# Up and gate products of six MLPs as seven block products (Strassen) in place of eight

## The chip, the cores and the metric

The kernel runs on one core of one Trainium2 chip. The metric is the time of one execution in microseconds of device time. A profile of one execution stands beside the times; its rows are shown below.

## The reference

Four layers over 512 tokens of width 1024, in float32. The change touches the feed-forward parts only. Cut to these:

```python
# first two layers, i = 0, 1 (width of the MLP 4096)
h = _layer_norm(DN_ALPHA * h + y, ln1_g[i], ln1_b[i])
u = jnp.square(jax.nn.relu(h @ mlp_w1[i])) @ mlp_w2[i]
h = _layer_norm(DN_ALPHA * h + u, ln2_g[i], ln2_b[i])
h = h + jax.nn.sigmoid(h @ ple_gate_w[i]) * (p[i] @ ple_w[i])
...
# last two layers (width 2816), a gated MLP ahead of and behind the mixer
def _swiglu(x, w_gate, w_up, w_down):
    return (jax.nn.silu(x @ w_gate) * (x @ w_up)) @ w_down
x = x + MACARON * _swiglu(_rmsnorm(x, ffn1_norm), ffn1_w_gate, ffn1_w_up, ffn1_w_down)
```

So there are six stages of the kind: two plain MLPs and four gated ones. The mixers (attention, retention and others) lie between them and stay as they are.

## The kernel before

**Split products.** TensorE multiplies in a short float format (`float32r`). To keep float32 accuracy every operand is split into a high part (ScalarE copies it into that format) and a low part (the rest, value minus high part), and each product is three matmuls: high x high, low x high, high x low. `mm3` (lines 431 to 434) issues them. In the up and gate products (`fm`, lines 468 to 493; `fm_product`, lines 459 to 466) the weights are the stationary operand, 128 x 128, and x, transposed, moves with 512 tokens as columns: one PSUM bank holds 128 features of 512 tokens. In the down products (`tm`, lines 511 to 546) the activations are stationary and the weights move.

**Weights.** `weight_plan` lists all weight tiles in the order of use, 128 x 2048 numbers (1 MB) each as a rule: 256 features of 1024 inputs for up and gate, 512 outputs of 512 inputs for down. Tile j goes through slot j % 2 of the buffers `wraw`, `whi` and `wlo`. SyncE's queue loads it (`load`, lines 2694 to 2706) when the old tenant has been split; ScalarE writes the high part (line 1065) when TensorE has used tile j - 2; GpSimd writes the low part (line 2541), and of a few tiles VectorE writes half (line 1652). `Slots.prepare` does this one tile ahead (`LOOK = 1`): the split of tile j + 1 has the time in which TensorE works on tile j.

**An MLP stage.** The hidden width is cut into chunks of 8 tiles of 128 features (`chunks`); the last chunk of the gated MLP has 6. For a chunk, first all up (and gate) products are made, then its down products, whose sum is added to the residual `h` by VectorE (lines 1761, 1763). Plain MLP: ScalarE applies relu on the way out of PSUM (line 1367), VectorE squares (line 2110), ScalarE makes the high part `uh` (line 1371), VectorE the low part `ul` (line 2112). Gated MLP: ScalarE applies silu to the gate's bank (line 1409), VectorE multiplies by the up product's bank (line 2150), then high part (line 1414) and low part (line 2152).

**Start of a stage.** The normed x has to be transposed: TensorE transposes 128 tokens (line 451), ScalarE and VectorE write `xh` and `xl` (lines 1084, 1701). `Handover` orders this around the last products of the stage before. So that work can start early, the first two weight tiles (four feature tiles) are multiplied with tokens 0 to 255 first and with 256 to 511 after that, as matmuls with 256 columns.

**The per-layer input.** GpSimd loads `p` (line 2603) at the start of a plain MLP, ScalarE and VectorE split it after the first chunk (lines 1381, 2122), and its products (`ple`) stand right behind the last down product; they cover the norm.

All engines run in the order in which their program issues; waits are semaphore waits written by name (`at(...)`).

Of the kernel before, what the change touches and what calls it, by code (L numbers as in the profile page):

```python
# [19 lines left out]
SLOT = 2048  # L20
NRAW, NSPL, LOOK = 2, 2, 1
# [13 lines left out]
FINAL = 13  # L35

# [74 lines left out]
class Slots:  # L111


    def __init__(self, plan, split):
        self.plan, self.split, self.i, self.ahead = plan, split, 0, 0

    def prepare(self):
        while self.ahead <= min(self.i + LOOK, len(self.plan) - 1):
            self.split(self.ahead)
            self.ahead += 1  # L120

    def get(self, tag, later=0):
        assert self.plan[self.i + later][0] == tag, (self.plan[self.i + later][0], tag)
        self.prepare()
        return self.i + later
# [64 lines left out]

def weight_plan(I):

    plan, shared = [], {0}
# [5 lines left out]
    def add_fm(tag, v, c0, c1, step=256):  # L199
        for c in range(c0, c1, step):  # L200
            plan.append((tag, v[:, :, c:min(c + step, c1)]))

    def add_tm(tag, v, c0, c1, early=False):
        nk = v.shape[1]
        for c in range(c0, c1, 512):
            for k, kn in k_parts(nk):
                plan.append((tag, v[:, k:kn, c:min(c + 512, c1)]))
        if early:
            n = len(plan) - 2
# [4 lines left out]
    plan.append(("e_g", v[:, :, 3328:3424]))  # L214
    add_fm("e_vs", v, 1024, 1280)
    for j in range(2):
        plan.append(("cmp", I["e_b_cmp_w1"][j].rearrange("p (k c) -> p k c", c=128)))
        add_fm("e_qk", v, 1280 + 256 * j, 1536 + 256 * j)
        shared.add(len(plan) - 1)
    n = len(plan)  # L220
# [4 lines left out]

    def plan_mlp(i):
        v1, v2 = kview("mlp_w1", i), kview("mlp_w2", i)
        parts = chunks(DFF // 128)
        for a, b in parts:
            add_fm("up", v1, a * 128, b * 128)  # L230
# [4 lines left out]
    def plan_glu(g, u, d, l):  # L235
        vg, vu, vd = kview(g, l), kview(u, l), kview(d, l)
        parts = chunks(DFF2 // 128)
        for a, b in parts:
            for c in range(a, b, 2):
                add_fm("glu", vg, c * 128, c * 128 + 256)  # L240
                add_fm("glu", vu, c * 128, c * 128 + 256)
            add_tm("down", vd[:, a:b, :], 0, D, (a, b) == parts[-1])

# [9 lines left out]
    for l in range(2):  # L253
        plan_glu("ffn1_w_gate_2", "ffn1_w_up_2", "ffn1_w_down_2", l)
# [6 lines left out]
        plan_glu("ffn2_w_gate_2", "ffn2_w_up_2", "ffn2_w_down_2", l)  # L261
    return plan, shared
# [6 lines left out]
def memory(nc, k):  # L269
# [13 lines left out]
    k.hi = [sb(f"whi{i}", [128, SLOT], R) for i in range(NSPL)]  # L283
    k.lo = [sb(f"wlo{i}", [128, SLOT], R) for i in range(NSPL)]
# [28 lines left out]
    def mlp(i):  # L313
        with ExitStack() as sc:
            def tmp(name, shape, dt=F):
                return sc.enter_context(nc.sbuf_tensor(f"{name}_m{i}", shape, dt))
            s = Kit()
            s.uh, s.ul = tmp("uh", [128, 8, T], R), tmp("ul", [128, 8, T], R)
            s.sg, s.pb = tmp("sg", [128, 4, 512]), tmp("pb", [128, 4, D])
            s.tb = tmp("tb", [128, 3, T])  # L320
            s.ph, s.pl = tmp("ph", [128, 2, T], R), tmp("pl", [128, 2, T], R)
            s.pr = tmp("pr", [128, 2, T])
            if i == 0:
                s.posi, s.posf, s.ang = tmp("posi", [128, NT], I32), tmp("posf", [128, NT]), tmp("ang", [128, 3, NT, 48])
# [26 lines left out]
    def glu(l, which):  # L351
        with ExitStack() as sc:
            def tmp(name, shape, dt=F):
                return sc.enter_context(nc.sbuf_tensor(f"{name}_g{l}{which}", shape, dt))
            s = Kit()
            s.uh, s.ul = tmp("uh", [128, 8, T], R), tmp("ul", [128, 8, T], R)
            s.tb = tmp("tb", [128, 4, T])
            return s

# [19 lines left out]
    k.mlp = {0: mlp(0)}  # L379
    k.odd = odd()  # L380
    k.zt = sb("zt", [128, 2, D])
    k.mlp[1] = mlp(1)
    k.glu = {(l, w): glu(l, w) for l in range(2) for w in (1, 2)}
# [3 lines left out]
def signals(nc, k, v):  # L387
# [8 lines left out]
    for n in range(NRAW):  # L396
# [3 lines left out]
def slot_views(k, j):  # L400
    kt, c = k.plan[j][1].shape[1:]
    return [x[j % NSPL][:, 0:kt * c].rearrange("p (k c) -> p k c", c=c) for x in (k.hi, k.lo)]


def split_views(k, j):
    kt, c = k.plan[j][1].shape[1:]
    return k.raw[j % NRAW][:, 0:kt * c], k.hi[j % NSPL][:, 0:kt * c], k.lo[j % NSPL][:, 0:kt * c]


def whole(k, j):  # L410
    return k.plan[j][0] == "cmp"


def glu_slots(a, b):
    return [(c, part) for c in range(a, b, 2) for part in ("g_gate", "g_up")]


def tensor_program(nc, k):
# [4 lines left out]
    slots = Slots(k.plan, lambda j: None)  # L423
# [7 lines left out]
    def mm3(o, lh, ll, rh, rl, start, stop):  # L431
        M.matmul(o, lh, rh, start=start, stop=False)  # L432
        M.matmul(o, lh, rl, start=False, stop=False)  # L433
        return M.matmul(o, ll, rh, start=False, stop=stop)  # L434

    def weights(j):
        pe.wait_ge(at("lo", j))
# [16 lines left out]
    def turned(tt):  # L454
        pe.wait_ge(at("xl", ho.round, tt))
# [38 lines left out]

    def tm_part(j, kr, bank, key, tt, src, nk, need, n, turns=True, last=False):
# [4 lines left out]
        for kk in range(*kr):  # L500
            if need:
                pe.wait_ge(at(*need(kk)))
# [76 lines left out]
    def even():  # L579
# [20 lines left out]
        def hidden(n):  # L600
            j = slots.get("cmp")
            pe.wait_ge(at("raw", j))
            pe.wait_ge(at("windows", n))
            w = k.raw[j % NRAW][:, 0:SLOT].rearrange("p (k c) -> p k c", c=128)
# [152 lines left out]

    def mlp(i):
        s = k.mlp[i]
# [2071 lines left out]
```

## Time and profile before

| | |
|---|---|
| Runs | 3649.26 us median of three (3648.98 to 3652.57) |
| Profiled execution | 3641.17 us, its span 3639.8 us |
| TensorE | 3467.6 us busy, 95% |
| VectorE, ScalarE, GpSimd | 1290.6, 1076.8, 1225.0 us busy (35%, 30%, 34%) |
| Mean granted TensorE clock | 0.974 of full |
| DMA | 308 MB, 85 GB/s |

Matmuls overlap: each is listed from its start to its modelled end, so the pace is read from one start to the next. "PEld" are the loads of the stationary operand. A row of idle time names what ended it.

### The profile page before, as it was taken

What the parts mean: (1) busy time and instruction counts of PE and PEld (TensorE: products, weight loads), DVE (VectorE), ACT (ScalarE), POOL (GpSimd) and SP (SyncE); (2) the same over time, 40 slices, a digit from 0 to 9 for tenths busy, and PEclk for the clock granted to TensorE, in tenths of its full rate; (3) what the DMA queues carried; (4) which work ended last, traced back from release to release, by engine and by line L of the source; (5) the groups of instructions that cost most, each with busy time, mean ns of one, the idle gap of its engine ahead of it and who ended that gap; (6) DMA issues with size and microseconds to landing.
All of it is one profiled execution on the core that took longest, in us unless ns stands there. A gap on an engine that the chain in (4) does not pass through costs nothing.

```text
span 3639.8 us, 37569 instructions
## 1 busy us (share of the span) xinstructions
PE 3467.6 (95%) x16220; PEld 2795.4 (77%) x16220; DVE 1290.6 (35%) x2250; ACT 1076.8 (30%) x1431; POOL 1225.0 (34%) x343
## 2 busy tenths in 40 slices
PE   7999999999879999999999999999999999999998
PEld 6775688887655888877888777888788877778887
DVE  3446533244682522252111546111221115461112
ACT  3453322223432232243222222222232222223222
POOL 3210134432421344423443332344334433323442
PEclk9989999999879999999999999999999999999999
DMA  4210123322110233222232321223222323222222
GB/s 155 85 47 1 37 97 97 112 78 91 52 41 25 86 104 104 93 87 81 93 109 82 105 93 58 93 93 110 82 93 93 98 84 117 77 70 93 93 99 81
DMA packets 221142, 308.33 MB, mean 85 GB/s; under 512 B 6096, under 2 KB 149472, under 8 KB 220464
## 3 DMA queue, kind: packets, MB, share of 16 engines
q1 hardware_dynamic: 217920, 293.50, 25.0%
q0 software_dynamic: 3056, 12.42, 0.9%
q8 instruction: 128, 2.10, 0.2%
q14 instruction: 38, 0.31, 0.0%
HBM read 303.80 MB, written 2.10 MB: 84 GB/s over the span
## 4 chain that ended last, share of the span: by engine, by line
PE 83%; DVE 11%; ACT 3%; POOL 2%; issue 1%; DMA 0%; ACTq 0%; DVEq 0%; POOLq 0%
PE bank L432 25%; PE bank L434 25%; PE bank L433 25%; ACT whi L1065 2%; POOL wlo L2541 2%; PE bank L734 1%; PE bank L705 1%; DVE wkk_o L2290 1%; DVE uv_x L2419 1%; PE bank L908 1%; DVE wlo L1652 1%; DVE gb L2287 1%; PE bank L719 1%; PE bank L451 1%; DVE tb_m L2110 1%
## 5 line engine op out<-in xcount | busy, mean ns | idle before, releaser
L2541 POOL TENSOR_TENSOR wlo<-wraw,whi 128x2048 fp32r<-128x2048 f32 (+2 forms) x279 | 1186.9, 4254 | 2189.4 <-ACT whi L1065 2189.4
L432 PE MATMUL bank<-xh,whi 128*128 128x512 f32 (+1 forms) x2456 | 922.6, 376 | 52.7 <-POOL wlo L2541 19.8
L434 PE MATMUL bank<-xh,wlo 128*128 128x512 f32 (+1 forms) x2456 | 917.7, 374 | 0.0
L433 PE MATMUL bank<-xl,whi 128*128 128x512 f32 (+1 forms) x2456 | 917.5, 374 | 0.0
L1065 ACT ACTIVATE whi<-wraw 128x2048 fp32r<-128x2048 f32 (+1 forms) x279 | 519.4, 1861 | 885.5 <-PE bank L434 854.2
L432 PEld LDWEIGHTS bank<-xh,whi 128*128 128x128 f32 x2456 | 466.9, 190 | 150.0 <-POOL wlo L2541 32.0
L434 PEld LDWEIGHTS bank<-xh,wlo 128*128 128x128 f32 x2456 | 466.7, 190 | 90.0
L433 PEld LDWEIGHTS bank<-xl,whi 128*128 128x128 f32 x2456 | 467.2, 190 | 88.7
L432 PE MATMUL bank<-whi,xh 128*128 128x512 f32 (+2 forms) x976 | 377.9, 387 | 22.7 <-POOL wlo L2541 9.6
L433 PE MATMUL bank<-wlo,xh 128*128 128x512 f32 (+2 forms) x976 | 371.6, 381 | 0.0
L434 PE MATMUL bank<-whi,xl 128*128 128x512 f32 (+2 forms) x976 | 371.1, 380 | 0.0
L1763 DVE SCALAR_TENSOR_TENSOR h<-bank,h 128x512 f32<-128x512 f32 x160 | 110.5, 690 | 588.1 <-PE bank L434 588.1
L2150 DVE TENSOR_TENSOR tb_g<-tb_g,bank 128x512 f32<-128x512 f32 x88 | 60.4, 687 | 716.2 <-PE bank L434 713.5
L432 PE MATMUL bank<-whi,uh_g 128*128 128x512 f32 x704 | 274.7, 390 | 5.6 <-POOL wlo L2541 5.6
L434 PE MATMUL bank<-whi,ul_g 128*128 128x512 f32 x704 | 274.0, 389 | 0.0
L433 PE MATMUL bank<-wlo,uh_g 128*128 128x512 f32 x704 | 273.9, 389 | 0.0
L432 PEld LDWEIGHTS bank<-whi,xh 128*128 128x128 f32 x976 | 188.7, 193 | 64.6 <-POOL wlo L2541 13.1
L434 PEld LDWEIGHTS bank<-whi,xl 128*128 128x128 f32 x976 | 188.1, 193 | 36.2
L433 PEld LDWEIGHTS bank<-wlo,xh 128*128 128x128 f32 x976 | 188.5, 193 | 34.3
L432 PE MATMUL bank<-whi,uh_m 128*128 128x512 f32 x512 | 199.9, 390 | 2.1 <-POOL wlo L2541 1.8
L434 PE MATMUL bank<-whi,ul_m 128*128 128x512 f32 x512 | 199.3, 389 | 0.0
L433 PE MATMUL bank<-wlo,uh_m 128*128 128x512 f32 x512 | 199.2, 389 | 0.0
(344 smaller groups left out, 3318.4 us busy)
## 6 DMA issues: line engine op xcount, KB each, us to landing
wraw<-in_mlp_w SPq DMA_DIRECT2D x64, 1024.0 KB, 5.3
wraw<-in_ffn_w_gate SPq DMA_DIRECT2D x44, 1024.0 KB, 5.4
wraw<-in_ffn_w_up SPq DMA_DIRECT2D x44, 1024.0 KB, 5.4
wraw<-in_ffn_w_down SPq DMA_DIRECT2D x40, 1024.0 KB, 5.1
wraw<-in_w_in SPq DMA_DIRECT2D x26, 1024.0 KB, 5.2
wraw<-in_e_w_in SPq DMA_DIRECT2D x13, 1024.0 KB, 5.5
wraw<-in_ple_gate_w SPq DMA_DIRECT2D x8, 1024.0 KB, 5.4
wraw<-in_w_out SPq DMA_DIRECT2D x8, 1024.0 KB, 5.0
```

Source lines behind the costliest of these rows:

```text
L432: M.matmul(o, lh, rh, start=start, stop=False)
L433: M.matmul(o, lh, rl, start=False, stop=False)
L434: return M.matmul(o, ll, rh, start=False, stop=stop)
L451: i = M.transpose(bank[:, j * 128:(j + 1) * 128], src[:, (f + j) * 128:(f + j + 1) * 128], ident)
L705: M.matmul(bank[:, 0:nk], lq, e.kvT[ps, 1 + br, 0:nk], start=True, stop=False)
L719: ins = M.transpose(bank[0:w, o:o + 128], e.P[:, (n % 2) * 2 + h, kk:kk + w], ident)
L734: ins = M.matmul(o[:, 0:256], lhs, rhs, start=(br == 0), stop=(br == 2 and kk + 128 >= nk))
L908: M.matmul(bank[:, 0:nk], o.qr[ps, hh // 2, s], o.krT[ps, 0:nk], start=False, stop=False)
L1065: A.activation(hi, raw, ACT.Copy).then_inc(*k.w_hi.inc(("hi", j)))
L1763: V.scalar_tensor_tensor(x, y, scale_y, x, ALU.mult, ALU.add).then_inc(*done.inc(*names))
L2150: V.tensor_tensor(t, t, ring.of(key)[:, :], ALU.mult).then_inc(*done.inc(("gu", g, f), ("free", key)))
L2541: G.tensor_tensor(lo[:, 0:n], raw[:, 0:n], hi[:, 0:n].bitcast(F), ALU.subtract).then_inc(*k.w_lo.inc(("lo", j)))
```

## The change

For a block of 2n feature tiles, x is cut into four quarters (two halves of the 1024 inputs by two halves of the 512 tokens) and the weights into four (two halves of the inputs by two of the features). Seven products of sums of quarters replace the eight products of quarters, in Winograd's form. A *unit* is one such block: n is 2 (four feature tiles), and 1 for the last two tiles of the gated MLP. Each of the seven products of a unit is n x 4 x 3 matmuls with 256 columns.

- *Sums of x* are made once for each stage, after all its tokens are transposed: `operands()` on VectorE (four sums, five low parts) and ScalarE (high parts). There are now seven operand pairs `x[0..6]`.
- *Sums of weights*: VectorE, in place in the raw buffer, four for each unit (`weight_sum`). The low parts of five of the seven weight operands move to VectorE; GpSimd keeps products 2 and 3 (and 1 in the two first units of a stage).
- *Buffers*: high and low buffers are four halves of 1024 columns, one for each product; a whole slot (down weights and all others) takes two. There are two more raw buffers while an MLP stage runs.
- *Partial sums* stay in PSUM where the next product adds to them. ScalarE copies a bank out in between (`snap`), and VectorE adds the later bank to the copy (`add_bank`).
- *Square* moves from VectorE to ScalarE. The load of `p` moves behind the last low part of `u`.

```diff
+OPERAND = {1: 4, 2: 5, 3: 3, 4: 6, 5: 0, 6: 1, 7: 2}
+SNAP = {1: "11", 5: "22", 6: "12"}
+SUM = {2: "11", 7: "22", 3: "12"}
+ON_POOL = (2, 3)
+def product_order(n, start):
+    steady = [(u, p) for u in range(n) for p in (1, 5, 6, 2, 7, 3, 4)]
+    if not start:
+        return steady
+    return [(0, 1), (0, 2), (1, 1), (1, 2), (0, 5), (0, 6), (1, 5), (0, 7), (1, 6), (0, 3), (0, 4), (1, 7), (1, 3), (1, 4)] + steady[14:]
...
 class Slots:
     def prepare(self):
-        while self.ahead <= min(self.i + LOOK, len(self.plan) - 1):
+        while self.ahead < len(self.plan) and max(self.plan[self.ahead].before, default=-1) < self.i:
...
+    def item(self, tag, load, n, unit=None, p=None):
+        if n == 2:
+            self.half += self.half % 2
+        halves = [(self.half + i) % 4 for i in range(n)]
+        self.half = (self.half + n) % 4
+        before = sorted({self.split_at[x] for x in halves if x in self.split_at})
...
+    def unit_sizes(a, b):
+        return [(f, 2 if f + 4 <= b else 1) for f in range(a, b, 4)]
...
 # TensorE
+    def units(tag, blocks):
...
+        for n, (i, p) in enumerate(product_order(len(blocks), start)):
+            u = blocks[i]
+            j = slots.get(tag)
+            wh, wl = weights(j)
+            if start and p not in (1, 2):
+                pe.wait_ge(at("operand", ho.round, p))
+            if p in (6, 7, 3):
+                pe.wait_ge(at("snap", u.key, {6: 1, 7: 6, 3: 5}[p]))
+            elif p == 4:
+                pe.wait_ge(at("sum", u.key, "22"))
+            key = ("bank", u.key, {5: "b", 3: "b", 2: "c"}.get(p, "a"))
...
+            for m in range(u.n):
+                for kk in range(4):
+                    ins = mm3(bank[:, m * 256:m * 256 + 256], wh[:, kk, m * 128:m * 128 + 128], wl[:, kk, m * 128:m * 128 + 128],
+                              hi[:, kk, :], lo[:, kk, :], p in (1, 5, 2) and m + kk == 0, (m, kk) == (u.n - 1, 3), True)
...
+            if start and n in (1, 2):
+                ho.turn(n + 1)
...
 # ScalarE
-        act.wait_ge(at("raw", j))
-        before = k.split_before(j)
-        if before is not None:
+        act.wait_ge(at("sum of", j) if item.p in (4, 5, 6, 7) else at("raw", item.load.n))
+        for before in item.before:
             act.wait_ge(at("used", before))
...
+            def finish(u, c):
+                t = s.t[order.index(u) % 2][c][:, 0:256 * u.n]
+                if c != "21":
+                    act.wait_ge(at("sum", u.key, c))
+                    A.activation(t, t, ACT.Relu).then_inc(*done.inc())
+                act.wait_ge(done.now())
+                A.activation(t, t, ACT.Square).then_inc(*done.inc())
...
-            if q == 0:
-                act.wait_ge(at("pr", i))
-                A.activation(s.ph[:, :, :], s.pr[:, :, :], ACT.Copy).then_inc(*done.inc(("ph", i)))
+        act.wait_ge(at("pr", i))
+        A.activation(s.ph, s.pr, ACT.Copy).then_inc(*done.inc(("ph", i)))
...
 # VectorE
+        if item.unit and not on_pool(item):
+            raw, hi, lo = split_views(k, item)
+            dve.wait_ge(at("hi", j))
+            V.tensor_tensor(lo, raw, hi.bitcast(F), ALU.subtract).then_inc(*k.w_lov.inc(("lo", j)))
...
+        if j + 1 < len(k.plan.items) and k.plan.items[j + 1].p in (4, 5, 6, 7):
+            weight_sum(j + 1)
...
+    def operands():
+        w, r = k.wide, ho.round
+        a, b, c, d = w.x32
...
+        V.tensor_tensor(w.s1, c, d, ALU.add).then_inc(*done.inc(("sum of x", r, 5)))
+        dve.wait_ge(done.now())
+        V.tensor_tensor(w.s2, w.s1, a, ALU.subtract).then_inc(*done.inc(("sum of x", r, 6)))
+        V.tensor_tensor(c, a, c, ALU.subtract).then_inc(*done.inc(("sum of x", r, 7)))
+        low_operand(5, w.s1)
+        dve.wait_ge(at("sum of x", r, 6))
+        V.tensor_tensor(b, b, w.s2, ALU.subtract).then_inc(*done.inc(("sum of x", r, 3)))
+        low_operand(6, w.s2)
+        low_operand(7, c)
+        low_operand(3, b)
...
+    def add_bank(u, p, t):
+        key = ("bank", u.key, {2: "c", 7: "a", 3: "b"}[p])
+        dve.wait_ge(at("product", u.key, p))
+        dve.wait_ge(at("snap", u.key, {2: 1, 7: 5, 3: 6}[p]))
+        V.tensor_tensor(t, t, ring.of(key)[:, 0:256 * u.n], ALU.add).then_inc(*done.inc(
+            ("sum", u.key, SUM[p]), *([("free", key)] if p != 7 else [])))
```

## Rows read from the trace of the kernel before

**Rows 1.** The page: busy time of the engines; the chain that ended last

```profile
PE 3467.6 (95%) x16220; PEld 2795.4 (77%) x16220; DVE 1290.6 (35%) x2250; ACT 1076.8 (30%) x1431; POOL 1225.0 (34%) x343
...
PE bank L432 25%; PE bank L434 25%; PE bank L433 25%; ACT whi L1065 2%; POOL wlo L2541 2%; PE bank L734 1%; PE bank L705 1%; DVE wkk_o L2290 1%; DVE uv_x L2419 1%; PE bank L908 1%; DVE wlo L1652 1%; DVE gb L2287 1%; PE bank L719 1%; PE bank L451 1%; DVE tb_m L2110 1%
```

**Rows 2.** Busy time by stretch (columns in the first line), steady gated MLP

```profile
core 0: us, PE busy (x) PEld busy (x) DVE busy (x) ACT busy (x) POOL busy (x), PEclk, DMA share, GB/s
2300.00:2372.00 72.00, 72.00 (x311) 58.11 (x311) 9.33 (x14) 19.76 (x20) 27.68 (x6) 1.00 0.31 101
```

**Rows 3.** Timeline (start us, us), TensorE, 512 columns: first and thirteenth matmul

```profile
2301.01 0.39 PE L432 MATMUL bank<-xh,whi 128*128 128x512 f32 x1
...
2303.81 0.39 PE L432 MATMUL bank<-xh,whi 128*128 128x512 f32 x1
```

**Rows 4.** Timeline, TensorE, 256 columns: first and twenty-fifth matmul, and a weight load

```profile
2268.22 0.28 PE L432 MATMUL bank<-xh,whi 128*128 128x256 f32 x1
2268.22 0.19 PEld L433 LDWEIGHTS bank<-xl,whi 128*128 128x128 f32 x1
...
2271.04 0.28 PE L432 MATMUL bank<-xh,whi 128*128 128x256 f32 x1
```

**Rows 5.** Groups by line and form, TensorE, whole span: busy us, mean ns

```profile
L432 PE MATMUL bank<-xh,whi 128*128 128x512 f32 x1936 | 769.6, 398 | 21.3 <-DVE xl L1834 12.3 <-POOL wlo L2541 8.6 <-ACT rl_o L1181 0.2
...
L432 PE MATMUL bank<-xh,whi 128*128 128x256 f32 x512 | 149.9, 293 | 31.4 <-DVE mv L1675 12.2 <-POOL wlo L2541 11.2 <-DVE wlo L1652 8.0
```

**Rows 6.** Groups by line and form, ScalarE: weights, a bank, a tile in SBUF

```profile
L1065 ACT ACTIVATE whi<-wraw 128x2048 fp32r<-128x2048 f32 x262 | 500.7, 1911 | 873.5 <-PE bank L434 842.2 <-DMA wraw<-in_e_w_in 11.6 <-DMA wraw<-in_w_in 9.7
...
L1181 ACT ACTIVATE tb_g<-bank 128x512 f32<-128x512 f32 x88 | 52.2, 598 | 287.2 <-PE bank L434 287.1
L1371 ACT ACTIVATE uh_m<-tb_m 128x512 fp32r<-128x512 f32 x64 | 40.4, 632 | 111.3 <-DVE tb_m L2110 111.3
...
L1065 ACT ACTIVATE whi<-wraw 128x1024 fp32r<-128x1024 f32 x14 | 14.8, 1057 | 8.0 <-PE bank L434 8.0
```

**Rows 7.** Groups by form, VectorE; two lines' durations (ns min/median/max), VectorE and GpSimd

```profile
L2150 DVE TENSOR_TENSOR tb_g<-tb_g,bank 128x512 f32<-128x512 f32 x88 | 60.4, 687 | 716.2 <-PE bank L434 713.5 <-ACT tb_g L1181 2.7
...
L2112 DVE TENSOR_TENSOR ul_m<-tb_m,uh_m 128x512 fp32r<-128x512 f32 x64 | 44.3, 692 | 44.7 <-ACT uh_m L1371 44.7
...
L1819 DVE TENSOR_TENSOR PT_x<-PT_x,k_x 128x256 f32<-128x256 f32 x16 | 6.8, 425 | 0.6
...
L1652 DVE TENSOR_TENSOR wlo<-wraw,whi x52: 684/1225/3411, 8.2 to 3615.3; 128x1024 fp32r<-128x1024 f32 x43, 128x512 fp32r<-128x512 f32 x8, 128x784 fp32r<-128x784 f32 x1
...
L2541 POOL TENSOR_TENSOR wlo<-wraw,whi x279: 1288/4610/4932, 8.2 to 3615.2; 128x2048 fp32r<-128x2048 f32 x109, 128x1024 fp32r<-128x1024 f32 x25, 128x512 fp32r<-128x512 f32 x4, 128x768 fp32r<-128x768 f32 x1
```

**Rows 8.** Timeline, GpSimd and VectorE, first plain MLP

```profile
487.42 4.61 POOL L2541 TENSOR_TENSOR wlo<-wraw,whi 128x2048 fp32r<-128x2048 f32 x1 [5.08 <-ACT whi L1065]
487.86 4.71 DVE L2110 TENSOR_TENSOR tb_m<-tb_m 128x512 f32<-128x512 f32 x1 [1.59 <-ACT tb_m L1181]
```

**Rows 9.** Start of the second gated MLP: timeline of TensorE, and a stretch

```profile
2643.55 0.36 PE L432 MATMUL bank<-xh,whi 128*128 128x256 f32 x1 [3.55 <-DVE mv L1675]
...
2645.80 0.41 PE L432 MATMUL bank<-xh,whi 128*128 128x256 f32 x1
2646.01 0.41 PE L433 MATMUL bank<-xl,whi 128*128 128x256 f32 x1
...
2653.45 0.38 PE L432 MATMUL bank<-xh,whi 128*128 128x256 f32 x1 [1.62 <-POOL wlo L2541]
...
2645.00:2655.00 10.00, 8.38 (x59) 8.14 (x59) 5.36 (x8) 3.30 (x4) 3.30 (x1) 0.84 0.33 105
```

**Rows 10.** The per-layer input: its load (KB, us to landing) and its two splits

```profile
pr_m<-in_pT POOLq DMA_DIRECT2D x2, 512.0 KB, 6.2
...
L1381 ACT ACTIVATE ph_m<-pr_m x2: 1037/1039/1041, 540.8 to 1298.1; 128x1024 fp32r<-128x1024 f32 x2
L2122 DVE TENSOR_TENSOR pl_m<-pr_m,ph_m x2: 1216/1216/1216, 550.4 to 1307.7; 128x1024 fp32r<-128x1024 f32 x2
```

**Rows 11.** Groups by line and form, ScalarE: table loads at the copies out of PSUM

```profile
L1181 ACT ACT_TABLE_LOAD x23 | 29.5, 1283 | 13.7 <-PE bank L434 13.3
```

More of the change, by code:

```diff
@@ L260, in weight_plan @@
         add_tm("l_out", kview("w_out_2", l), 0, D, True)
-        plan_glu("ffn2_w_gate_2", "ffn2_w_up_2", "ffn2_w_down_2", l)
-    return plan, shared
+        plan_glu("ffn2_w_gate_2", "ffn2_w_up_2", "ffn2_w_down_2", l, 2)
+    return plan, {j for j in shared if j < len(plan.items) and not plan.items[j].unit}, blocks
 class Kit:
@@ L349, in odd @@
             return s
[L351 to L358, printed above, removed]
     def mixer(l):
@@ L785, in glu @@
         for q, (a, b) in enumerate(parts):
-            fm("glu", [[(part, g, c), (part, g, c + 1)] for c, part in glu_slots(a, b)], x)
+            blocks = k.blocks["glu", g, a]
+            units("glu", blocks)
             if q == 1:
@@ L1136, in tm, with units, snap @@
                 slots.done()
+    def units(tag, blocks, product, finish):
+        start = bool(ho.pending or ho.moved or ho.half)
+        if start:
+            ho.turn(0)
+            ho.turn(1)
+        waiting = []
+        for n, (i, p) in enumerate(product_order(len(blocks), start)):
+            slots.get(tag)
+            slots.done()
+            if start and n in (1, 2):
+                ho.turn(n + 1)
+                if n == 2:
+                    operands()
+            product(blocks[i], p)
+            while waiting:
+                finish(*waiting.pop(0))
+            if p in (2, 7, 3, 4):
+                waiting.append((blocks[i], {2: "11", 7: "22", 3: "12", 4: "21"}[p]))
+        while waiting:
+            finish(*waiting.pop(0))
+    def snap(u, p, dst, *free):
+        act.wait_ge(at("product", u.key, p))
+        for event in free:
+            act.wait_ge(event)
+        src = ring.of(("bank", u.key, "b" if p == 5 else "a"))[:, 0:256 * u.n]
+        A.activation(dst[:, 0:256 * u.n], src, ACT.Copy).then_inc(*done.inc(("snap", u.key, p)))
     def residual(key, c, tt):
@@ L1416, in glu @@
+            units("glu", k.blocks["glu", g, a], product, finish)
             if q == 1:
@@ L2727, in build @@
     k.I, k.out, k.at, k.landed = I, out, values.at, {}
-    k.plan, k.shared = weight_plan(I)
-    def split_before(j):
-        old = [i for i in range(max(0, j - 3 * NSPL), j) if i % NSPL == j % NSPL and not whole(k, i)]
-        return old[-1] if old else None
-    k.split_before = split_before
+    k.plan, k.shared, k.blocks = weight_plan(I)
     k.ring = Ring(nc)
```

513 lines of the change are left out of this document (372 added, 141 removed).

## The prediction

> **What bounds the kernel now.** I read the share of busy time first, then the chain that ended last: TensorE works in 95% of the span, and three quarters of the chain are the three matmuls of the split product [rows 1]. In a steady stretch of a gated MLP no time is left on it at all, while VectorE is busy 9.3 us of 72 and GpSimd 27.7 [rows 2]. So the time falls only with TensorE's work, and VectorE has room. How much work goes is a question of pace, not of the duration of one matmul, which overlaps the next: I read starts. In 512-column products 12 matmuls start in 2.80 us, 233.3 ns each [rows 3]; in the first block of a stage, which already works on 256 tokens at a time, 24 start in 2.82 us, 117.5 ns each, each with a weight load of its own [rows 4]. Half the columns cost half the time, and the new products are all of that form.
>
> **What is removed.** The up and gate products are 2 x 32 and 4 x 44 tiles of 128 features, each 8 x 3 matmuls: 5760 of 512 columns. Of these, 4 tiles in each of 6 stages are done today in halves, 1152 matmuls of 256 (384 of each of the three lines, of the 512 in [rows 5]; the other 5184 are 1728 of each of the 1936). Today: 5184 x 0.2333 + 1152 x 0.1175 = 1345 us. Strassen leaves 7/8 of the columns, all as 256-column matmuls: 5760 x 2 x 7/8 = 10080 x 0.1175 = 1184 us. **Gain 160 us.** The row decides here. The Trainium skill (TensorE: Matmul & The Clock Gate, Back-to-back issue gap) gives N/2.4 + 2.5 ns, 109 and 216 ns; the trace's starts are 8% further apart, and by that rule the gain would be 142 us.
>
> **What each product now costs the others.** A unit of two tiles by two ("n=2") has 7 products of 24 matmuls, 2.82 us a product, 19.7 us a unit. Durations [rows 6, 7]: ScalarE 1.06 us for a half slot of weights, 0.60 for a bank, 0.63 for a tile in SBUF; VectorE 1.23 for 128x1024, 0.69 for 128x512, 0.43 for 128x256; GpSimd on the line through its shortest 128x512 (1.29) and median 128x2048 (4.61): 2.4 for 128x1024.
> - VectorE, a unit of the plain MLP: 4 weight sums and 5 low parts x 1.23, 3 bank sums and 4 low parts of u x 0.69 = 15.9 us of 19.7. A gate-up pair: 18 x 1.23 + 14 x 0.69 = 31.8 of 39.5, but 18.7 of 19.7 in the up unit.
> - ScalarE, plain MLP: 7 x 1.06 + 4 x 0.60 + 11 x 0.63 = 16.7 of 19.7; a pair 23.4 of 39.5.
> - GpSimd 2 x 2.4 a unit. It seems free, but it isn't: a VectorE op with both inputs in SBUF stood 4.71 us, 0.69 of work, behind a GpSimd instruction that began 0.44 us earlier, and both ended together with it [rows 8]. Ops of 512 that read a bank keep 0.69 on average [rows 7]. The Trainium skill (SBUF — State Buffer, Who interferes with whom) says the same: two SBUF inputs contend with GpSimd's reads, and who issues first holds the ports for the whole instruction. The trace agrees.
>
> All of it has a lead: an item's high part may begin when the item four before it is used, so splits run three products (8.5 us) ahead. I followed one unit through the FIFO queues. With no lock the sum "22", for which product 4 waits on TensorE, is ready 1.4 us (plain) or 0.9 us (up unit) before it is needed, so nothing stalls. Products 6, 3 and 7 also wait, for ScalarE's copy of a bank (0.60 us); a whole product lies between, so I cost them at nothing; without that cover it would be 0.6 us each and ScalarE's queue ahead of it, up to 3 us. Behind a waiting matmul stand only the unit's own later ones; behind VectorE's wait for a product's end stand the low parts of the next weights, and TensorE waits for those. GpSimd's two ops fall into products 1 and 6, VectorE's light part, except after an up unit, whose backlog of 3 us still runs there: two locks push the low part of product 7's weights 1.4 us past its start. **Steady loss**: 12 plain units x 0.4, 16 pairs x 0.8, and 4 pairs of the half-size units (18 x 0.69 + 14 x 0.43 = 18.4 us of VectorE and 5.2 of locks in 19.7 us) x 2 = 26 us. Bounds: 0, and 60 if each lock hits.
>
> **Into the down product.** Its first weights are a full slot, two halves, the second of which comes free only with the third product from the end: two products' lead, 5.6 us, for 1.91 us on ScalarE and 4.61 on GpSimd [rows 6, 7]. Today a slot has 11.2 us. 16 times 0.9 us at least; I take 1.5, as GpSimd may wait for one VectorE op. After the half-size units, 4 times, the lead is 2.8 us: 3.7 to 4.3. **41 us**, bounds 29 and 60.
>
> **Start of a stage.** Today TensorE waits 3.55 and 1.62 us there [rows 9]. The first wait stays. New: after tokens 256 to 511 are turned, VectorE makes four sums and five low parts of x (11.1 us) before it serves weights again, and TensorE has one product (2.8 us) meanwhile. Followed through: the first operand comes 3.4 us late, the next weights 2.5, then 0.8: 6.7 us in place of 1.6, **30 us** for 6 stages; bounds 12 and 60. What is late next is VectorE's weights, not ScalarE.
>
> **The per-layer gate input.** Its load moves from the start of the stage behind the last low part of u: 6.2 us to landing, then 1.04 and 1.22 [rows 10], after a 1.06 and a 1.29 us split. TensorE has 5.6 us of matmuls and 1.9 of transposes left: 3.3 us late, twice, **7 us**; 0 to 16. ScalarE waits for the load ahead of the turn of the last tokens, which are not late for that: the products of this input come first and cover them. The weights' bytes stay the same; their shorter loads and more issues on SyncE are hidden: the DMA engines are 31% busy [rows 2], and two units' halves lie between a load and its use. 448 products bring more semaphore waits; satisfied ones leave no gap between the slots of today, so nothing.
>
> **Clock.** After a wait of 3.5 us the granted clock of the next 10 us is 0.84, matmuls of 256 columns start 0.21 us apart and not 0.12, and some 1.6 us are lost [rows 9]. Waits that long come in some 5 more places: **8 us**, 0 to 16.
>
> **Sum.** 160 - (26 + 41 + 30 + 7 + 8) = 160 - 112 = 48 us. The profiled execution took 3641.2 us (span 3639.8), the median of the runs is 3649.3: 3593 against the profile, **3601** against the median. 0.2%, 7 us, is about what a measurement of this kernel can tell from no change.
>
> **Rivals.**
> - *All of it hides* (0.18). The leads swallow the locks and only the two unavoidable terms are left, 29 and 12 us: 160 - 41 = 119 us, 3530. For it: VectorE has 87% idle time in steady stretches now. Against: the lock [rows 8] and the 5.6 us lead.
> - *Slower: VectorE becomes the bound* (0.15). In one place: VectorE's queue in the steady units. If each of GpSimd's ops blocks it for its whole length (31.8 + 9.6 = 41.4 us a pair) and it also waits some 2 us a unit at the head of its queue for ScalarE's high parts, a pair takes 45.4 in place of 39.5, a plain unit 22.7, a half-size pair 6 more: 20 x 5.9 + 16 x 3 + 4 x 6 = 190 us, starts included; with 41 + 7 + 8 elsewhere 246, against a gain of 160: 86 us slower, 3735. It decides from a steady loss of 74 us on, 1.5 us a unit. The rule on the ports cited above is what would bring it about; against it stands that two of seven products alone use GpSimd.
> - *The square moves to ScalarE with a table load* (0.05). Loads take 1.28 us [rows 11]; the trace has none between Relu and Copy, and Square isn't in it. Two for each of 64 squares would make ScalarE's unit 26.9 us of 19.7: 115 us more, about 3716. The Trainium skill (ScalarE: Activation LUTs, Table sets) names relu and copy as present in every set and is silent on square there.
>
> **How the numbers follow.** The forecast has 0.62, with an own range of 3560 to 3640. 3530 to 3665 takes in the first rival and the upper bounds of the terms where they don't all fall together (160 - 145, and a little more), and leaves out the two slow rivals. Faster 0.79 (forecast and first rival, less the forecast's worst end), same 0.04, slower 0.17.
>
> **What would show it.** Matmuls 10080 of 256 columns starting 117 to 118 ns apart; a steady pair of units 39.5 to 41 us; TensorE's waits named VectorE's low weights and operands at six starts, GpSimd's low weights at 20 entries into the down products; VectorE busy 80% in gate-up stretches with single ops of 2 to 3.5 us. I am wrong if the 256-column pace is over 125 ns when it lasts for whole stages, if VectorE is over 95% busy there, or if the waits into the down products are missing.

## The result: 0.75% slower, where 1.3% faster was forecast

| | before | after |
|---|---|---|
| Median of 5 runs each, same chip | 3648.98 us (3643.76 to 3652.57) | 3675.65 us (3667.77 to 3683.13) |
| Ratio, 95% interval | | 1.0075 (1.0054 to 1.0095) |
| Span of the profiled execution | 3639.8 us | 3674.4 us |
| TensorE busy, idle | 3467.6, 172.2 us | 3379.6, 294.8 us |
| Mean granted clock | 0.974 | 0.956 |

The page of the changed kernel, its busy time and its chain, against [rows 1]:

```profile
PE 3379.6 (92%) x19964; PEld 2928.2 (80%) x19964; DVE 2129.9 (58%) x2970; ACT 1464.0 (40%) x2085; POOL 1062.6 (29%) x363
...
PE 71%; DVE 15%; ACT 7%; POOL 3%; issue 3%; DMA 0%; DVEq 0%; ACTq 0%; POOLq 0%
PE bank L579 21%; PE bank L581 21%; PE bank L580 21%; POOL wlo L2917 3%; ACT whi L1253 3%; DVE wlo L1924 2%; PE bank L915 1%; PE bank L886 1%; DVE raw_w L1945 1%; DVE wkk_o L2665 1%; DVE wraw L1945 1%; DVE uv_x L2794 1%; PE bank L900 1%; PE bank L1096 1%; DVE gb L2662 1%
```

Three lines carry the reading. TensorE did lose work, but 88 us where I had counted 160. Its idle time grew by 122.6 us. VectorE has 839 us more to do and holds 15% of the chain.

What TensorE waited for (us in total, times, longest), after:

```profile
PE bank L579 <- POOL wlo L2917: 79.5, 38, 6.9
PE bank L579 <- DVE xl L2028: 44.4, 6, 8.9
PE bank L579 <- ACT zt L1378: 18.1, 6, 3.3
PE bank L579 <- DVE al_w L2484: 14.3, 2, 7.2
...
PE bank L579 <- DVE zt L2107: 4.5, 8, 0.6
PE bank L579 <- ACT zt L1625: 3.8, 2, 1.9
PE bank L579 <- DVE t_w L2522: 3.5, 4, 0.9
```

and the two lines of before that answer to the first two (L1652 is the low part of the next weights, for which TensorE waited at the starts):

```profile
PE bank L432 <- POOL wlo L2541: 36.7, 21, 6.9
...
PE bank L432 <- DVE wlo L1652: 8.3, 6, 2.9
```

L2028 is the low part of an operand sum, L1378 the copy of a bank (`snap`), L2484 the low part of `p`. The first row grew by 43 us, the others are new, and 8.3 us of before are gone: together that is the growth of 122.6 us but for a few tenths. L1625 is the square: TensorE waits for it at the first entry into down of each plain MLP.

Stretches of the same work, before. In order: a chunk of a gated MLP, from the first down product of one chunk to that of the next; the same for a plain MLP; the start of a gated MLP; the start of the first plain MLP; and all that lies ahead of the first MLP, where no product is changed.

```profile
2359.80:2493.00 133.20, 133.20 (x578) 108.06 (x577) 16.57 (x24) 31.95 (x28) 55.82 (x13) 1.00 0.30 93
...
594.40:682.75 88.35, 88.35 (x386) 72.01 (x385) 23.87 (x27) 25.00 (x25) 37.89 (x10) 1.00 0.33 108
...
2266.00:2359.00 93.00, 91.16 (x493) 77.78 (x494) 25.52 (x29) 27.59 (x30) 34.40 (x9) 1.00 0.30 97
...
452.00:506.00 54.00, 49.41 (x308) 43.90 (x306) 32.79 (x30) 17.28 (x23) 17.03 (x6) 0.97 0.27 88
...
0.00:452.00 452.00, 411.59 (x2027) 305.12 (x2028) 230.45 (x588) 179.77 (x392) 76.82 (x32) 0.94 0.20 65
```

and after (the columns are those of [rows 2]):

```profile
2408.10:2533.60 125.50, 123.88 (x865) 115.96 (x865) 76.41 (x73) 52.01 (x60) 40.01 (x13) 1.00 0.31 101
...
705.87:794.64 88.77, 85.31 (x528) 77.12 (x528) 44.59 (x41) 39.38 (x49) 29.93 (x8) 0.98 0.29 95
...
2309.50:2408.10 98.60, 85.11 (x688) 84.38 (x688) 82.78 (x75) 51.38 (x65) 28.97 (x10) 0.95 0.26 86
...
462.70:525.30 62.60, 46.53 (x354) 45.01 (x353) 53.11 (x46) 37.16 (x52) 21.15 (x7) 0.89 0.20 68
...
0.00:462.70 462.70, 422.47 (x2027) 311.89 (x2028) 230.98 (x589) 182.17 (x398) 75.79 (x32) 0.91 0.21 68
```

Read down the first columns: the gated MLP's chunk gains 7.7 us, the plain MLP's chunk loses 0.4, and both starts lose (5.6 and 8.6 us). The start of a gated MLP has VectorE busy for 82.8 of 98.6 us, where it was 25.5 of 93. The last row of each fence lies outside the changed stages: ahead of the first of them TensorE does the same 2027 matmuls, but is busy for 10.9 us more, at a clock of 0.91 for 0.94, and the first MLP begins 10.7 us later. The three stretches of mixers between the MLPs give 7.2 us back (229.6, 116.0 and 116.0 us before, 225.6, 114.4 and 114.4 after). So of the 34.6 us between the two spans some 31 lie in the stretches with the MLPs.

**A start, from close.** Timeline after, start of the second gated MLP (start us, us, engine, line, and in brackets the idle time before and its releaser):

```profile
2313.04 5.75 POOL L2917 TENSOR_TENSOR wlo<-wraw,whi 128x1024 fp32r<-128x1024 f32 x2 [1.37 <-ACT whi L1253]
...
2313.19 3.35 DVE L1983 SCALAR_TENSOR_TENSOR zt<-h,rs,gb 128x1024 f32<-128x1024 f32 x1
2316.46 3.42 DVE L1945 TENSOR_TENSOR raw_w<-raw_w 128x1024 f32<-128x1024 f32 x1
...
2319.91 1.06 ACT L1253 ACTIVATE whi<-raw_w 128x1024 fp32r<-128x1024 f32 x1 [5.52 <-DVE raw_w L1945]
2320.88 1.07 ACT L1290 ACTIVATE u_w<-bank 128x512 f32<-128x512 f32 x2
...
2326.94 1.22 DVE L2010 TENSOR_TENSOR u_w<-u_w 128x1024 f32<-128x1024 f32 x1
...
2331.84 0.55 PE L579 MATMUL bank<-xh,whi 128*128 128x256 f32 x1 [8.91 <-DVE xl L2028]
...
2345.95 0.35 PE L579 MATMUL bank<-xh,whi 128*128 128x256 f32 x1 [2.66 <-ACT zt L1378]
```

Two GpSimd operations block two of VectorE: with both inputs in SBUF, VectorE's stand while GpSimd's run (a lock, as in [rows 8]), and 1.28 and 1.22 us of work become 3.35 and 3.42. ScalarE stands 5.5 us for the weight sum, with the copies of the last turned tokens (L1290) behind it, so the sums of x begin at 2326.94 and TensorE restarts at 2331.84, 8.9 us late. It waits once more 14 us later, for a snap.

**An entry into down in the plain MLP**, same view:

```profile
691.02 3.43 DVE L1945 TENSOR_TENSOR wraw<-wraw 128x1024 f32<-128x1024 f32 x1
...
699.29 1.90 ACT L1253 ACTIVATE whi<-raw_w 128x2048 fp32r<-128x2048 f32 x1
...
701.27 4.54 POOL L2917 TENSOR_TENSOR wlo<-raw_w,whi 128x2048 fp32r<-128x2048 f32 x1 [7.91 <-ACT whi L1253]
...
705.87 0.50 PE L579 MATMUL bank<-whi,uh_w 128*128 128x512 f32 x1 [3.49 <-POOL wlo L2917]
```

A lock (3.43 us for 1.22 of work) on a weight sum makes VectorE's bank sum late, with it ScalarE's relu, square and high part of that tile, and behind those stands the high part of the down weights. Of GpSimd's 4.54 us 3.5 are in the open.

**The per-layer input**, same view:

```profile
835.54 2.07 ACT L1275 ACTIVATE xh<-bank 128x512 fp32r<-128x512 f32 x4 [3.71 <-PE bank L599]
837.46 1.08 ACT L1253 ACTIVATE whi<-raw_w 128x1024 fp32r<-128x1024 f32 x1
...
838.62 1.80 POOL L2917 TENSOR_TENSOR wlo<-raw_w,whi 128x512 fp32r<-128x512 f32 x1 [14.79 <-ACT whi L1253]
840.36 0.75 POOL L2990 DMA_DIRECT2D t_w<-in_pT  x1
...
849.44 0.79 PE L579 MATMUL bank<-whi,ah_w 128*128 128x512 f32 x1 [7.17 <-DVE al_w L2484]
```

The load is issued at 840.36, because it stands on GpSimd's queue behind the low parts of the next weights, and GpSimd had waited 14.8 us for the last of them. That one's high part came late in its turn: on ScalarE's queue it stands behind the copies of turned tokens (L1275). The load landed 6.5 us later.

### The profile page after: what moved, and what is told of

It reads as the page before. It is cut to its first block, busy times and chain, and to the rows that moved or that the text cites. A ratio compares the mean times of both kernels' runs of the same rounds, so it can differ in the third digit from the quotient of the medians.

```text
span 3674.4 us, 47176 instructions
## 1 busy us (share of the span) xinstructions
PE 3379.6 (92%) x19964; PEld 2928.2 (80%) x19964; DVE 2129.9 (58%) x2970; ACT 1464.0 (40%) x2085; POOL 1062.6 (29%) x363
## 4 chain that ended last, share of the span: by engine, by line
PE 71%; DVE 15%; ACT 7%; POOL 3%; issue 3%; DMA 0%; DVEq 0%; ACTq 0%; POOLq 0%
PE bank L579 21%; PE bank L581 21%; PE bank L580 21%; POOL wlo L2917 3%; ACT whi L1253 3%; DVE wlo L1924 2%; PE bank L915 1%; PE bank L886 1%; DVE raw_w L1945 1%; DVE wkk_o L2665 1%; DVE wraw L1945 1%; DVE uv_x L2794 1%; PE bank L900 1%; PE bank L1096 1%; DVE gb L2662 1%
## 5 line engine op out<-in xcount | busy, mean ns | idle before, releaser
L2917 POOL TENSOR_TENSOR wlo<-wraw,whi 128x2048 fp32r<-128x2048 f32 (+3 forms) x182 | 646.4, 3553 | 1449.1 <-ACT whi L1253 1437.6
L579 PE MATMUL bank<-xh,whi 128*128 128x256 f32 (+1 forms) x2264 | 675.4, 298 | 98.6 <-DVE xl L2028 44.4
L1253 ACT ACTIVATE whi<-wraw 128x1024 fp32r<-128x1024 f32 (+2 forms) x336 | 431.0, 1284 | 773.3 <-PE bank L581 588.9
L581 PE MATMUL bank<-xh,wlo 128*128 128x256 f32 (+1 forms) x2264 | 670.6, 296 | 0.0
L580 PE MATMUL bank<-xl,whi 128*128 128x256 f32 (+1 forms) x2264 | 666.4, 294 | 0.0
L579 PE MATMUL bank<-whi,uh_w 128*128 128x512 f32 x1216 | 485.7, 399 | 56.6 <-POOL wlo L2917 52.5
L580 PE MATMUL bank<-wlo,uh_w 128*128 128x512 f32 x1216 | 481.8, 396 | 0.0
L581 PE MATMUL bank<-whi,ul_w 128*128 128x512 f32 x1216 | 480.6, 395 | 0.0
L579 PE MATMUL bank<-ah_w,whi 128*128 128x256 f32 x1440 | 411.4, 286 | 14.8 <-POOL wlo L2917 5.2
L580 PE MATMUL bank<-al_w,whi 128*128 128x256 f32 x1440 | 408.9, 284 | 0.0
```

Of the source, the lines that this page charges most:

```text
L579: M.matmul(o, lh, rh, start=start, stop=False, skip_group_check=more)
L580: M.matmul(o, lh, rl, start=False, stop=False, skip_group_check=more)
L581: return M.matmul(o, ll, rh, start=False, stop=stop, skip_group_check=more)
L1253: A.activation(hi, raw, ACT.Copy).then_inc(*k.w_hi.inc(("hi", j)))
L2917: G.tensor_tensor(lo[:, 0:n], raw[:, 0:n], hi[:, 0:n].bitcast(F), ALU.subtract).then_inc(*k.w_lo.inc(("lo", j)))
```

## Experiments

Each kernel was timed beside the kernel before on the same chip; where two kernels that were not timed side by side are compared, it is by their ratios to before (a ratio of 0.001 is 3.6 us), whose intervals are some 0.002 to either side.

The theory after the comparison: (1) the start of a stage is bound by VectorE's work and its locks, not by the order in which it is issued; (2) the first down block comes late because its low part is one long GpSimd operation; (3) `p` comes late because its load is issued late; (4) the short waits also cost clock (no run tests this one alone). The rival for all: the new products themselves are dearer than their pace in [rows 4].

**Matmuls of 256 columns alone** (before, all up and gate products in two halves):

```diff
-                fm_product(j, m, take(key), key, src, slice(0, T), nk, need, m == len(these) - 1)
+                fm_product(j, m, bank, (*key, "first"), src, slice(0, 256), nk, need, False)
+                fm_product(j, m, bank, key, src, slice(256, T), nk, need, m == len(these) - 1)
```

> Edit of the kernel before: all up and gate products, not only the first four tiles of a stage, are done in two halves of 256 columns, no Strassen. It measures the pace of 256 columns by itself: 10368 matmuls in place of 5184. If they start 117.5 ns apart as in the short stretches of before: 1218 against 1209 us, 9 us more, 3658. If a long run of them is slower (the rival on the pace, 120 ns or more): 35 us more or above, 3684.

Measured: 3644.36 us, ratio to before 0.9999 (0.9984 to 1.0013), with 21404 matmuls in place of 16220. The page's first row:

```profile
PE 3468.7 (95%) x21404; PEld 3035.6 (83%) x21404; DVE 1290.2 (35%) x2250; ACT 1076.9 (30%) x1431; POOL 1223.9 (34%) x343
```

TensorE's busy time is that of before to 1.1 us. The form costs nothing, not even the 9 us expected from the rows of before; the rival falls, but for a small part. In the changed kernel products whose moving operand lies in `xh` keep that pace, those in `ah` are slower. Timeline, first matmul of three products of 24:

```profile
2457.51 0.28 PE L579 MATMUL bank<-xh,whi 128*128 128x256 f32 x1
...
2460.34 0.28 PE L579 MATMUL bank<-ah_w,whi 128*128 128x256 f32 x1
...
2463.22 0.28 PE L579 MATMUL bank<-xh,whi 128*128 128x256 f32 x1
```

2.83 us, then 2.88: 0.118 and 0.120 us a matmul, and so it is on average over all products at the full clock (213 with `xh`, 130 with `ah`: 117.9 and 120.1 ns). With 4 and 3 of the 7 products, 10080 matmuls take some 12 us more than at 0.1175.

**The order at the start** (ScalarE and VectorE turn the last tokens and make the operands ahead of the next weights, not behind):

```diff
-            slots.get(tag)
-            slots.done()
             if start and n in (1, 2):
                 ho.turn(n + 1)
                 if n == 2:
                     operands()
+            slots.get(tag)
+            slots.done()
```

> Edit of the changed kernel: at the start of a stage ScalarE and VectorE turn the last tokens and make the sums of x ahead of the next weights' sums and splits, and not behind them. Theory A (queue order: ScalarE stands at the high part of product 5's weights, which waits for VectorE's sum behind two GpSimd locks, and the turned tiles stand behind it): TensorE's wait for the first operand (44.4 us in 6 stages, up to 8.9 each) falls to 3 to 4 us each, and the half-speed stretch after it goes: 30 to 45 us less, about 3635. Theory B (VectorE has too much to do in the start block, in whatever order): the wait moves to the next products' weights and the time stays within 8 us of 3676.

Measured: 3676.59 us, ratio to before 1.0094 (1.0076 to 1.0111), no better than the changed kernel (1.0075). Its waits:

```profile
PE bank L579 <- DVE xl L2028: 29.7, 6, 6.0
...
PE bank L579 <- DVE wlo L1924: 11.6, 9, 2.3
```

The operand waits fall by 14.7 us, and 10.8 us of them come back as waits for the low parts of weights (0.8 us in the changed kernel). What is served first only decides who waits: order is not the cause.

**The entry into down** (the first block's low part halved between GpSimd and VectorE):

```diff
+        if tag == "down":
+            shared.add(len(plan.items))
```

> Edit of the changed kernel: the low part of the first weights of each down product is shared by GpSimd and VectorE, a half each. Theory A (lead of two products too short for 1.91 us on ScalarE and 4.6 us on GpSimd, made worse by the clock that falls behind it): TensorE's waits for GpSimd's low weights fall from 79.5 us to 36 to 45, some 8 half-speed stretches go: 35 to 50 us less, about 3634. Theory B (VectorE is the bound in these stages, each op more on it costs): 20 ops of 1.2 us more, the time stays or rises by up to 24 us.

Measured: 3643.05 us, ratio 0.9998 (0.9986 to 1.0009): 28 us faster than the changed kernel by the ratios, 33 by the medians, a little under what was expected; and the waits fall to 58.1 us, not to 36 to 45. The wait, and two stretches, a plain and a gated chunk:

```profile
PE bank L581 <- POOL wlo L2919: 58.1, 31, 8.4
```

```profile
698.60:784.60 86.00, 83.70 (x528) 75.98 (x528) 44.83 (x42) 39.41 (x48) 28.80 (x8) 1.00 0.30 98
2390.70:2515.00 124.30, 123.78 (x866) 115.94 (x865) 75.98 (x74) 52.01 (x60) 38.86 (x13) 1.00 0.32 102
```

This plain chunk falls from 88.8 to 86.0 us and its clock goes from 0.98 to 1.00: in the changed kernel all five waits of 3.5 us at such entries are followed by matmuls at 1.2 GHz (clock 0.58 to 0.64 over the next 4 to 5 us), here the waits are 2.3 us and that still happens behind three of the five. Behind the eight waits of 1.1 us of the changed kernel's gated chunks it stays at 1.00. The gated chunk falls by 1.2 us. With both edits (order and entry):

> Both edits (start order, shared first down weights). Theory A: the two gains add, 65 to 95 us less than the changed kernel, 3580 to 3610, which is under the kernel before. Theory B: no gain beyond the larger of the two alone.

Measured: 3641.93 us, ratio 1.0000 (0.9985 to 1.0014): the order adds nothing here either.

The control, the same edit in the kernel before:

> The kernel before, with the low part of each first down block shared between GpSimd and VectorE in the same way: the control for that edit. In the kernel before, TensorE waits at the entries into down for 1.3 us once in the first plain MLP and for about 1 us in the gated ones. If the edit mends something that the seven products brought, the time stays within 0.2% of 3645; if it is worth as much here (33 us), the edit had nothing to do with the change.

Measured: 3641.12 us, ratio 0.9995 (0.9983 to 1.0007). The edit mends only what the change had brought.

**The per-layer input early** (load between the first and the second down block on GpSimd's queue, splits behind the fourth eviction):

```diff
             slots.skip("up", 7 * len(blocks))
-            slots.skip("down", 4)
+            slots.skip("down", 1)
+            if b == DFF // 128:
+                for u in blocks:
+                    for c in ("11", "22", "12", "21"):
+                        pool.wait_ge(at("ul", u.key, c))
+                G.dma_start(s.pr, I["pT"][i].rearrange("(k p) t -> p k t", p=128)).then_inc(*k.landed["ple"].inc(("pr", i)))
+            slots.skip("down", 3)
```

> The changed kernel with the per-layer input taken early: GpSimd issues its load as soon as the last u tiles are made, between the first and the second block of the last down weights in place of after all four, and its high and low parts stand behind the fourth eviction of the last down stage in place of behind all eight. If the wait at that place is what it seems (TensorE waits 7.2 us for the low part, twice, and runs at 1.2 GHz behind it), the kernel is about 18 us faster than the changed kernel (some 3658 against 3676), and the two waits at the low part of p are gone. If the wait only hides another (the x update, the operands' turn), the time stays within 3 us of 3676.

Measured: 3658.17 us, ratio to before 1.0050 (1.0031 to 1.0069): 9 us under the changed kernel by the ratios, 17.5 by the medians, 12.9 by the spans (3661.5 against 3674.4). The 18 us expected are met by the medians alone, and that is in part luck: the first MLP begins 6.7 us earlier than in the changed kernel (first matmul at 457.18 for 463.84), in code that the edit does not touch. The two stretches with the plain MLPs are 5.9 and 4.4 us shorter. The waits at `p` are gone from its table, but idle time falls by 8.5 of their 14.3 us (3661.5 - 3375.2 = 286.3, against 294.8): waits of 1 us for the eviction and of a few tenths for low parts and snaps come in. The place is shown, its full price isn't.

**Without the weight sums** (products 4 to 7 take the quarter as it was loaded, so the kernel computes something else; it leaves out 256 operations of VectorE):

```diff
-        V.tensor_tensor(b, a, b, ALU.subtract).then_inc(*done.inc(("sum of", j)))
+        done.so_far(("sum of", j))
```

> The changed kernel without the sums of weight quarters on VectorE (products 4 to 7 take the quarter as it was loaded, so what they compute is something else; no instruction of TensorE, ScalarE or GpSimd is left out). That is 4 operations of 0.6 to 1.1 us per unit, some 160 to 180 us of VectorE's work. If VectorE's throughput is what holds the starts of the stages and the entries into down, the operand waits fall from 44 us to under 15, the snap waits (18 us) go, and the kernel comes out at 3625 to 3645. If what holds them is the order in which ScalarE and GpSimd do their work and the locks between GpSimd and VectorE, it stays above 3660.

Measured: 3601.48 us, ratio to before 0.9884 (0.9866 to 0.9902), 70 us under the changed kernel, and more than the 30 to 50 expected. Its waits and a plain chunk:

```profile
PE bank L579 <- DVE xl L2028: 22.9, 6, 4.8
...
PE bank L579 <- ACT zt L1378: 2.9, 5, 1.0
```

```profile
681.40:766.20 84.80, 83.72 (x529) 76.01 (x529) 30.04 (x33) 39.16 (x49) 28.12 (x8) 1.00 0.31 100
```

Operand waits halve, the snap waits fall from 18.1 to 2.9, and the plain chunk gains 4.0 us. TensorE, ScalarE and GpSimd issue the same instructions, so it was the sums on VectorE that held them: their time in its queue, and ScalarE's wait for each; the run does not part the two. The half of the operand waits that stays (22.9 us, where under 15 were expected) is not the sums'. Of the 82.4 us between the spans 11.2 lie ahead of the first MLP and are not the edit's.

**No GpSimd in the steady units** (all seven low parts on VectorE):

```diff
-ON_POOL = (2, 3)
+ON_POOL = ()
```

> The changed kernel with the low parts of all seven products' weights on VectorE and none on GpSimd. If the locks between GpSimd and VectorE (operations of 3.4 to 5.7 us in place of 1.1) cost more than the work itself, the kernel is faster than the changed one, 3650 to 3670. If VectorE's throughput decides (some 3 more operations of 1.1 us per unit of about 19.8 us, where it is busy for about 14), the time is the same in the steady units and the operand waits at the starts grow: 3680 to 3710.

Measured: 3686.27 us, ratio to before 1.0117 (1.0098 to 1.0136); 15 us slower than the changed kernel, as throughput says. But not where I said: the operand waits fell slightly, and the wait for GpSimd's first down block grew.

```profile
PE 3376.9 (92%) x19964; PEld 2926.2 (79%) x19964; DVE 2148.0 (58%) x3098; ACT 1467.0 (40%) x2085; POOL 723.4 (20%) x235
```

```profile
PE bank L579 <- POOL wlo L2917: 94.0, 44, 8.4
PE bank L579 <- DVE xl L2028: 41.0, 6, 8.4
```

VectorE has 128 operations more, 156 us of work at 1.22 us each, and is busy for only 18 us more. So the 128 GpSimd operations had cost it some 138 us of standing blocked, nearly as much as doing their work. And the operand waits hardly move (44.4 to 41.0): with the work on VectorE in the place of the locks the starts are as late.

**Two edits together** (entry and `p`):

> The changed kernel with two of the edits that gained alone: the low part of each first down block shared between GpSimd and VectorE (33 us alone), and the per-layer input taken early (17.5 us alone). If the two waits have nothing to do with each other, the gains add up: about 50 us under the changed kernel, some 3626, which is 15 us (0.4%) under the kernel before. If the clock gives the second gain only where the first is missing, it stays at 3638 to 3645.

Measured: 3630.11 us, ratio 0.9964 (0.9948 to 0.9979). By the ratios the gains of 28 and 9 become 40: they add up.

**Seven products in the gated MLPs alone** (the plain MLPs' code, plan and early load of `p` from before):

```diff
-WIDE = (1, 5, 7, 9, 10, 12)
+WIDE = (7, 9, 10, 12)
...
-            keys = [(("up", i, f), v1, f, n) for f, n in unit_sizes(a, b)]
-            blocks["up", i, a] = plan.units("up", keys, a == 0)
+            add_fm("up", v1, a * 128, b * 128)
```

> Seven products in the gated MLPs alone; the two plain MLPs as in the kernel before (eight products, per-layer input loaded early). By the chunk times of the two profiles the plain MLPs took 8.7 us more each at their start, 0.4 us more in each of 6 later chunks and 10 us more each at the per-layer input, 40 us in all, and gained nothing: theory A (the loss is in the plain MLPs' short chunks, their starts and their per-layer input) gives 3636, just under the kernel before. If the loss is spread over all stages (rival), it gives 3655 or more.

Measured: 3630.08 us, ratio 0.9958 (0.9943 to 0.9973). Theory A holds, with 6 us to spare; that the spare is clock behind the plain MLPs' waits is likely but not shown. And with the entry edit:

> As the kernel with seven products in the gated MLPs alone, with the low part of each first down block shared between GpSimd and VectorE. The chunks of the gated MLPs gained 1.1 to 1.2 us each by that (12 chunks, 14 us), so 3622 if that one comes out at 3636: 0.6% under the kernel before. If the plain MLPs gain by the sharing too, up to 12 us less.

Measured: 3611.66 us, ratio 0.9905 (0.9889 to 0.9922), faster than both kernels, 30 us under before by the medians. Its mean clock is 0.965. Its waits:

```profile
PE bank L583 <- POOL wlo L2903: 42.5, 21, 8.4
PE bank L583 <- DVE xl L2016: 27.3, 4, 8.9
```

The waits for GpSimd's low parts are back at 6 us over before. The four starts are not mended: 27.3 us for operands.

## Why the prediction was wrong

Its sum, term by term. Idle time is from the tables of waits; TensorE's busy time fell by 88 us where 160 - 12 = 148 was due, so 60 us are left over; they are put down to matmuls at half speed, which the count of half-speed time below bears out to some 55.

| term (us; of the sum, + is faster) | forecast | measured |
|---|---|---|
| gain by pace | 160 | 160 - 12 |
| steady units | 26 | 8 (4.5 + 3.5) |
| entries into down | 41 | 47 (79.5 - 36.7 + 3.8) |
| starts | 30 | 54 (44.4 + 18.1 - 8.3) |
| `p` | 7 | 14 |
| clock | 8 | 60 |
| sum | +48 | -35 |

- **Pace.** Right: the halves cost nothing by themselves. The small excess for `ah` was not seen from before, as that buffer did not exist. (The side sum of 142 us, from 109 and 216 ns, should read some 144 to 147; the forecast does not use it.)
- **Steady units.** Right in kind and too dear. A gated chunk has four units; at the forecast paces each saves 22.40 - 19.74 = 2.66 us, 10.6 in all, and less the forecast 3.1 of waits that made 7.5: it gained 7.7. That VectorE would become the bound in the steady units (the slower rival) did not happen: VectorE was busy 31.7 of 40 us there (2454 to 2494), the forecast 80%, while TensorE never stood still. In the whole chunk TensorE is idle for 1.6 us, of which the entry is 1.1. (In [rows 8] VectorE's operation ended 0.5 us after GpSimd's and not together with it, so it did most of its 0.69 us of work behind the lock.)
- **Entries.** Nearly right in sum, wrong in place. I gave 1.5 us to each of the 16, and had 4.3 for those behind half-size units. Wait by wait TensorE waits 57 us at the 20 entries, where it waited 7 us before. The eight of the gated MLPs' full chunks have 1.1 us each, the four behind half-size units 3.9 and 1.3. The eight of the plain MLPs have 27 together: 5.7 us once, 3.5 five times (by the chain shown above: the lock, ScalarE's queue, and 3.5 of GpSimd's 4.54 us in the open), and 1.9 twice for the square. Of that chain I had costed the lead, the split and a wait for one VectorE operation, not what a late bank sum does to ScalarE's queue.
- **The start of a stage failed most among the waits.** My step "the first operand comes 3.4 us late" left out that two locks fall there, that ScalarE's copies of the turned tokens stand behind a weight sum, and "so I cost them at nothing" of the snaps: 8.9 us and 2.7 us in the start shown, 7.4 and 3.0 on average, instead of 6.7 in all. The order edit shows that the queues' order is not the reason, the run without GpSimd in the steady units that taking the locks away for as much work of VectorE's own does not help, and the run without sums that the weight sums are half of it (44.4 to 22.9 us). For the other half VectorE's own sums and low parts of x are the likely cause; no run tested it.
- **`p`.** The chain was right, load and splits behind the last weights' 1.06 and 1.29 us, but the cover was not: "TensorE has 5.6 us of matmuls and 1.9 of transposes left". ScalarE's copies of turned tokens stood ahead of that high part, which began at 837.46, when TensorE had 4.8 us left (it stopped at 842.27), and the low part took 1.80 us: 7.2 us, not 3.3.
- **The clock is the term that decided the sign, and the step that failed most: "Waits that long come in some 5 more places", at 8 us.** With 8 in place of 60 the sum would be +17. Half-speed time is 2 x (1 - clock) x span, with the unrounded clocks of 0.9744 and 0.9556: 186 us before, 326 after. From the first MLP's start on there are 40 stretches at half speed in place of 16. Of the 40, 24 stand at waits that the change brought or lengthened: ten at the six starts (0.89 and 0.95 in the stretches above), the eight entries of the plain MLPs (0.98 of 88.8 us, 3.6 us at half speed each), the four entries behind half-size units and the two waits at `p`. The Trainium skill (TensorE: Matmul & The Clock Gate, Terms) puts the loss at the throttled time times one minus the clock's share, here a half: 140 more us would cost 70, less what falls into idle time. The trace agrees as far as it can tell: TensorE was busy in 110 of these 140 us, which makes 55, against the 60 left over above.
- Part of that is not in the changed stages: 11 of the 60 us are the busy time ahead of the first MLP (422.47 for 411.59 us). The first MLP's first matmul came at 450.1 to 453.7 us in the three profiled kernels without any seven products, and at 452.0 to 464.7 in the ten with them, although nothing ahead of it does seven products; each is one execution. The cause stays open, and no run was made for it. For the same reason the runs show the clock's share less well than the waits': with the entry edit TensorE's busy time falls by 7.0 us, 3.7 of them ahead of the first MLP, beside 24.8 us of idle time; without the weight sums it falls by 25.0, 11.4 of them ahead, beside 57.4.
- **The square** brought no table load: this is the third rival, and it is false. The view of that line shows no operation but the 64 squares (ns min/median/max), and the whole trace has 64 table loads before and after:

```profile
L1625 ACT ACTIVATE t_w<-t_w x32: 629/632/637, 492.0 to 1569.5; 128x512 f32<-128x512 f32 x32
L1625 ACT ACTIVATE zt<-zt x32: 629/632/634, 510.4 to 1568.2; 128x512 f32<-128x512 f32 x32
```

The time of 3676 lies outside the range of 3530 to 3665. The prediction's own upper bounds, 60 + 60 + 60 + 16 + 16 = 212, would have given 3701; the range stopped at 3665 because the terms were not expected to fall together. But they had a common cause: a late VectorE operation made a wait, and behind waits such as the 3.5 us at an entry the matmuls ran at half speed. None of the three signs of being wrong came up (a pace over 125 ns, VectorE over 95% busy, no waits into down): not one of them looked at the clock.

## What to carry to other kernels

Taking an eighth of TensorE's up and gate work away paid here in the four gated stages, with 16 tiles between two entries, and not in the two plain ones, with 8, which gave it back at their entries, starts and `p` (3630 with seven products in all six and both edits, 3612 in the four alone with the entry edit). That the length between the entries makes the difference is my reading; no run varied it. Price each new wait with the clock behind it, and look at each queue in issue order for what a moved DMA stands behind. When work goes to VectorE, do not count on GpSimd to take a part of it for nothing: it blocked VectorE for nearly as long as that part would have taken there. Moving it all to VectorE was no better either (15 us slower): fewer operations are what helped.

## What the runs showed of the hardware

- Two VectorE operations in a row, 1.28 and 1.22 us of work, took 3.35 and 3.42 us beside a pair of GpSimd operations. The Trainium skill (SBUF — State Buffer, Who interferes with whom) has the lock; that it costs VectorE 138 us for 128 operations (1.1 us each) is what the run with an idle GpSimd adds.
- 5184 matmuls of 512 columns as 10368 of 256, each with a weight load of its own, took the same time.
- Products of the same form with their moving operand in another buffer ran at 0.120 in place of 0.118 us a matmul (means of 130 and 213 products). Not explained.
- Behind each of the five waits of 3.5 us TensorE ran at 1.2 GHz for a while, behind three of five waits of 2.3 us, and at 2.4 GHz behind all eight waits of 1.1 us.
